# A hybrid SSD, mLSTM and PEER layer on one core: the order of loads, evacuations, sample rows and closing norms at the seams between its stages

## What is computed

```python
proj = einsum('bld,dc->blc', x, w_in)              # one projection for all parts
z_s, xbc, dt_pre, u_m, v_m, o_m, i_pre, f_pre = split(proj)
xbc, new_ssd_conv = causal_conv(xbc, st_ssd_conv)  # 4 taps, then SiLU
y_s, h_new = ssd_scan(...)                         # chunks of 128 tokens, 16 heads of 64
y_s = rms_norm((y_s + d_skip * xs) * silu(z_s), ssd_norm_g)
u_c = silu(causal_conv(u_m, st_mconv)); q, k = u_c @ w_mq, u_c @ w_mk
num = att @ v + w_inter * (q @ c)                  # mLSTM, 4 heads of 256
den = att.sum + w_inter * (q @ n);  h = num / max(|den|, exp(-m_t))
h_m = sigmoid(o_m) * (layer_norm_per_head(h) * mlstm_norm_g)
mix = concat([y_s, h_m]) @ w_out
x1 = layer_norm(ALPHA * x + mix, ln1_g, ln1_b)
# PEER: 8 heads; two top-16 lists of 128 keys each, top 16 of their sums
#       = 16 experts of 16384 for each token and head, with softmax gates
hid = gelu(einsum('td,thkd->thk', x1, take(u, eidx)))
out = einsum('thk,thkd->td', gate * hid, take(v, eidx))
x2 = layer_norm(ALPHA * x1 + out, ln2_g, ln2_b)    # y; all updated states are outputs too
```

## Time and profile before

| what | us |
|---|---|
| runs of the kernel before | 3408.26, 3424.15, 3424.18 (median 3424.15) |
| the profiled execution | 3417.68, of it span 3415.8 |
| TensorE busy | 3118.2 (91%) |
| VectorE busy | 2546.0 (75%) |
| GpSimd busy | 1710.7 (50%) |
| ScalarE busy | 933.5 (27%) |
| moved by DMA | 1074.44 MB, 315 GB/s over the span |

### The profile page before, as it was taken

One profiled execution on the slowest core, in us unless ns is written; L12 is line 12 of the kernel. 1 busy time (PEld: TensorE's weight loads), 2 busy tenths in 40 slices (PEclk: granted clock), 3 DMA queues, 4 the chain that ended last, 5 costly groups with the idle time before them and its releaser, 6 DMA issues.

```text
span 3415.8 us, 42585 instructions
## 1 busy us (share of the span) xinstructions
PE 3118.2 (91%) x13811; PEld 2060.5 (60%) x13811; DVE 2546.0 (75%) x5375; ACT 933.5 (27%) x2140; POOL 1710.7 (50%) x1420
## 2 busy tenths in 40 slices
PE   8998999998888888889877658999999999999998
PEld 8997887787333233333244336767667766776774
DVE  6672044888397889998889977777777777777777
ACT  3212222665111121121178771111111111111111
POOL 3231221443036777777754556555555555555553
PEclk9999999999899999999989788999999999999999
DMA  4325465677568999999989999999999999999996
GB/s 147 98 70 171 155 222 191 228 266 286 205 205 314 358 379 373 389 380 358 369 323 348 338 351 392 391 385 395 372 386 396 369 387 378 392 402 388 391 394 240
DMA packets 385759, 1074.44 MB, mean 315 GB/s; under 512 B 55688, under 2 KB 145576, under 8 KB 379280
## 3 DMA queue, kind: packets, MB, share of 16 engines
q0 software_dynamic: 186624, 679.56, 52.5%
q1 hardware_dynamic: 149104, 309.77, 25.3%
q10 hardware_dynamic: 49824, 82.58, 6.5%
HBM read 978.55 MB, written 93.08 MB: 314 GB/s over the span
## 4 chain that ended last, share of the span: by engine, by line
PE 45%; DVE 11%; DMA 9%; issue 5%; POOL 2%; ACT 1%; SPq 0%; DVEq 0%; POOLq 0%; ACTq 0%
PE PB L2260 18%; PE PB L2247 14%; DMA vbf<-in_peer_v,gixv 5%; PE PB L2223 4%; PE PB L2287 3%; PE PB L2236 3%; DVE ub L1916 3%; DMA x1d<-in_peer_u 3%; PE PB L2205 1%; DMA ub<-in_peer_u,gix 1%; POOL vbf L1646 1%; DVE ohb L1863 1%; POOL ub L1646 1%; DVE oha L1861 1%; PE PB L2331 1%
## 5 line engine op out<-in xcount | busy, mean ns | idle before, releaser
L1646 POOL DMA_INDIRECT ub<-in_peer_u,gix x640 | 696.3, 1088 | 725.8 <-DVE hid L1916 525.5
L2260 PE MATMUL PB<-vbd,wd 128*128 128x512 f32 x1536 | 685.0, 596 | 0.0
L2247 PE MATMUL PB<-xds,uts 128*128 128x384 f32 x3072 | 569.5, 340 | 0.0
L2247 PEld LDWEIGHTS PB<-xds,uts 128*128 128x128 f32 x3072 | 531.8, 189 | 0.5 <-issue 0.5
L1646 POOL DMA_INDIRECT vbf<-in_peer_v,gix x340 | 396.4, 1166 | 167.1 <-issue 98.0
L2260 PEld LDWEIGHTS PB<-vbd,wd 128*128 128x128 f32 x1536 | 284.1, 192 | 309.6 <-issue 309.6
L2287 PE MATMUL PB<-vbf,dg 128*64 128x512 f32 x1200 | 319.1, 655 | 96.9 <-DMA vbf<-in_peer_v,gixv 92.2
L1646 POOL DMA_INDIRECT vbf<-in_peer_v,gixv x300 | 324.6, 1082 | 156.4 <-issue 85.0
L1877 DVE TENSOR_TENSOR uts<-PB,uts 128x512 fp32r<-128x512 f32 x256 | 175.6, 686 | 303.0 <-ACT uts L2093 302.7
L1916 DVE CUSTOM_DVE_ANT_0 ub<-ub,x1g 128x1024 f32<-128x1024 f32 x257 | 312.9, 1221 | 47.2 <-DMA ub<-in_peer_u,gix 37.8
L2093 ACT CAST uts<-PB 128x512 fp32r<-128x512 f32 x256 | 149.9, 586 | 646.9 <-PE PB L2236 635.3
(11 more groups left out here) (400 smaller groups left out, 5030.4 us busy)
## 6 DMA issues: line engine op xcount, KB each, us to landing
vbd<-in_peer_v SPq DMA_DIRECT2D x128, 512.0 KB, 6.9
x1d<-in_peer_u SPq DMA_DIRECT2D x96, 512.0 KB, 9.3
gd_d<-stag ACTq DMA_DIRECT2D x12, 2048.0 KB, 9.6
gbd<-gd_d SPq DMA_DIRECT2D x16, 1536.0 KB, 18.9
ubd<-in_peer_u SPq DMA_DIRECT2D x32, 512.0 KB, 10.1
wtr<-in_w_tok SPq DMA_DIRECT2D x6, 2048.0 KB, 9.2
tok_d<-stg ACTq DMA_DIRECT2D x48, 256.0 KB, 2.0
rb_e<-rows_d SPq DMA_DIRECT2D x8, 1536.0 KB, 10.7
```

The lines of the kernel that those rows point to most:

```text
L1646: pool.indirect_dma_start(out=buf, out_offset=None, in_=a[table], in_offset=bass.IndirectOffsetOnAxis(ap=index, axis=0)).then_inc(done, 16)
L2247: last = T.matmul(PB[:, 6, 0:TD], uts[:, b % 2, ul, k, :], xds[:, xl, k, :], start=(k, n) == (0, 0), stop=(k, n) == (KD - 1, 2))
L2260: last = T.matmul(PB[:, 2 * d + n, :], wd[:, b % 2, d * CH:(d + 1) * CH], vbd[b % 8][:, n * 512:(n + 1) * 512], start=b == 0, stop=b == NB ...
```

## The change

- **Projection:** SyncE issues the first two w_ch loads after the seventh piece of x. ScalarE's channel loop is put in another order: a half's evacuation stands ahead of the other half's SiLU.
- **Scan, samples:** one masked copy of the queries, `qsm`, makes `sample_num` give only sample n's row and zeros elsewhere, and VectorE adds the eight results into one tile, `numr` (`sample_sum`). The row stores, `num_d` and its load are gone. The samples' SSD part is gated, squared and scaled in channel layout in rounds 0 and 3; the mLSTM part is normalised in 4 x 32 partitions after the loop; both go to `mixt_d` as one store, over zeros stored in round 0. Ten loads instead of five precede `sample_start`.
- **Scan, chunk 0:** `mt0` holds all 16 rows and is loaded in round 3; all of chunk 0's mix is computed before the barrier. x, gain, bias, the first mix group of chunk 1 and the first four pieces of the score weights (`wp0`) are loaded there too, into tiles that keep their place in the next stage.
- **PEER, head:** rows 0 to 2 of chunk 1's mix stand ahead of the transposes; VectorE's constants stand behind the first norm; the other loads of `wp` are interleaved with the mix groups.
- **PEER, end:** a tile's sum comes out of the operation that makes it (`accum_out`); ScalarE makes the mean, and the variance by one Square pass; VectorE's norms are interleaved with the sums. Four of the samples' v gathers stand ahead of the last slots, eight small loads bring their x1 rows, and their product runs in four column groups.

The diff, cut to its core:

```diff
@@ projection, SyncE
-                    for q in range(2):
-                        sp.dma_start(wcr[q][:, :, :], a["w_ch"][q, :, :, :]).then_inc(s_w[q], 16)
                     for k in range(KD):
                         free(sp, s_xl, k - NX + 1)
                         sp.dma_start(xst[k % NX], a["x_t"][:, k, :]).then_inc(s_x[k % NX], 16)
+                        if k == KD - 2:
+                            for q in range(2):
+                                sp.dma_start(wcr[q][:, :, :], a["w_ch"][q, :, :, :]).then_inc(s_w[q], 16)
@@ projection, ScalarE (chan_out: evacuation and its two stores; chan_silu: SiLU and its two stores)
+                    chan_out(0, 0)
+                    for i in steps(act, NCT // 2 - 1):
+                        chan_out(i, 1)
+                        chan_silu(i, 0)
+                        chan_out(i + 1, 0)
+                        chan_silu(i, 1)
+                    chan_out(NCT // 2 - 1, 1)
+                    for q in range(2):
+                        chan_silu(NCT // 2 - 1, q)
@@ scan, SyncE, round 3 and the end
+                if i == 3:
+                    sp.wait_ge(s["stored"], 16)
+                    sp.dma_start(mt0[:, :, :], mixt_d[0]).then_inc(s["mt0"], 16)
...
+            sp.wait_ge(s["dve_mix"], NCH)
+            sp.dma_start(x1e[:, :], a["x_tok"][0:CH, :]).then_inc(s["x0"], 16)
+            sp.dma_start(g1e[:, :], a["ln1_g"].partition_broadcast(P)).then_inc(s["x0"], 16)
+            sp.dma_start(mte[:, 0, :, :], mixt_d[1, :, 0:4, :]).then_inc(s["mt1"], 16)
+            for j in range(4):
+                sp.dma_start(wp0[:, j, :, :], wp_d[j]).then_inc(s["wp0"], 16)
@@ scan, TensorE
-                pe.wait_ge(ss["ld"], 16 * 5)
+                pe.wait_ge(ss["ld"], 16 * 10)
...
+            first_mix(0, 4)
+            sample_num(NCH - 1, 0)
+            first_mix(4, 6)
             mix_transposes(pe, P, NCH - 1)
+            pe.wait_ge(ss["mix"], 1)
...
+            first_mix(6, 16).then_inc(s["mix0"], 1)
@@ scan, ScalarE, end
+            act.dma_start(mixt_d[NCH, :, :, 0:B], mixs[:, :, :], allow_slow_non_contiguous=True).then_inc(ss["stored"], 16)
@@ scan, VectorE
+            V.memset(onesq[:, :], 1.0)
+            for tile in (qsm, numr, orow, grow):
+                V.memset(tile[:, :], 0.0)
+            V.memset(emr[:, :], 0.0).then_inc(ss["zeroed"], 1)
             V.memset(v1[:, :, DK:DK + 1], 1.0).then_inc(s["setup"], 1)
...
+            def sample_sum(n, bank=2):
+                dve.wait_ge(ss["num"], n + 1)
+                if n:
+                    dve.wait_ge(ss["numc"], n)
+                V.tensor_tensor(numr[:, :], numr[:, :], PB[:, bank, 0:DK], ALU.add).then_inc(ss["numc"], 1)
@@ PEER, SyncE
-                load_mt(0, 3)
-                load_x(0)
...
-                for j in range(NHC):
+                sp.sem_inc(s["xr"], 16)
+                sp.sem_inc(s["gl1"], 16)
+                sp.sem_inc(s["gl2"], 16)
+                sp.sem_inc(s_mt[0], 16)
+                for j in range(4, 8):
                     load_wp(j)
                 load_mt(1, 1)
+                for j in range(8, 12):
+                    load_wp(j)
+                load_mt(1, 2)
+                for j in range(12, 16):
+                    load_wp(j)
                 load_x(1)
@@ PEER, TensorE
-                pe.wait_ge(s_wo[3], 16)
-                for j in range(12, 16):
-                    mix(0, j)
+                pe.sem_inc(s["mixg"], 1)
+                for j in range(3):
+                    mix(1, j)
                 transposes(0)
...
-                        for n in range(NSMP):
-                            pe.wait_ge(s_vs[n], 16)
+                        for r in (1, 0):
+                            for g in range(4):
+                                pe.wait_ge(s_vs[4 * r + g], 16)
                             for x in range(2):
+                                for g in range(4):
+                                    last = T.matmul(PB[32 * g:32 * g + 2, 6 + x, :], wgs[:, 4 * r + g, 0:2], (ub if r else vbf)[:, g, x * 512:(x + 1) * 512],
+                                                    start=r == 1, stop=r == 0, tile_position=(0, 32 * g))
@@ PEER, VectorE, end (last_norm: reciprocal and two scalar_tensor_tensor)
+                def last_sum(n, x, psum):
+                    V.scalar_tensor_tensor(x, x, ALPHA, psum, ALU.mult, ALU.add, accum_out=ends[:, n, 0:1]).then_inc(s["ends_sum"], 1)
...
                 for d in range(ND):
                     dve.wait_ge(s["g2"], NBLK + d)
+                    last_sum(1 + d, x1d[:, d, :], two(2 * d))
+                    if d == 1:
+                        last_norm(0, acc[GATHERED - 1])
+                last_norm(1, x1d[:, 0, :])
+                dve.wait_ge(s["xsr"], 16 * NSMP)
                 dve.wait_ge(s["go"], 1)
+                last_sum(1 + ND, x1[:, :], two(6))
+                for d in range(1, ND):
+                    last_norm(1 + d, x1d[:, d, :])
+                last_norm(1 + ND, x1[:, :])
@@ PEER, ScalarE, end
+                    S.activation(ends[:, n, 0:1], ends[:, n, 0:1], ACT.Copy, scale=-1.0 / D).then_inc(s["ends_mean"], 1)
+                    act.wait_ge(s["ends_mean"], 2 * n + 1)
+                    S.activation(work[:, 0:D], x, ACT.Square, bias=ends[:, n, 0:1], accum_out=ends[:, n, 1:2]).then_inc(s["ends_mean"], 1)
+                    act.wait_ge(s["ends_mean"], 2 * n + 2)
+                    S.activation(ends[:, n, 1:2], ends[:, n, 1:2], ACT.Sqrt, scale=1.0 / D, bias=epsc[:, :]).then_inc(s["ysq"], 1)
```

More of the change, by code:

```diff
@@ L650, in build @@
             wo = late.enter_context(nc.sbuf_tensor("wo", [P, 16, D], f32))
-            mt0 = late.enter_context(nc.sbuf_tensor("mt0", [P, 12, CH], f32))
+            wp0 = late.enter_context(nc.sbuf_tensor("wp_first", [P, 4, KD, NK], f32))
+            late.enter_context(nc.sbuf_tensor("late_gap", [P, MIX_GAP], f32))
+            first = [late.enter_context(nc.sbuf_tensor(n, shape, f32))
+                     for n, shape in (("mt", [P, 2, 4, CH]), ("x1", [P, D]), ("x1T", [P, KD, CH]), ("gb1", [P, D]), ("gb2", [P, D]))]
         with ExitStack() as ctx:
-            build_scan(nc, a, o, ctx, sem, PB, ident, two, wo, s_wo, s_pre, pre, mt0, cht_d, chs_d, ych_d, tok_d, rows_d, rows_s_d, mixt_d)
+            build_scan(nc, a, o, ctx, sem, PB, ident, two, wo, s_wo, s_pre, pre, wp0, first, wp_d, cht_d, chs_d, ych_d, tok_d, rows_d, rows_s_d, mixt_d)
         end_phase()
@@ L891, in sample_start @@
             def sample_start():
-                pe.wait_ge(ss["ld"], 16 * 5)
+                pe.wait_ge(ss["ld"], 16 * 10)
+                for j in range(8):
+                    last = T.transpose(PB[:, 4, j * B:(j + 1) * B], z_s.rearrange("b j n -> b (j n)")[:, j * P:(j + 1) * P], ident[0:B, 0:B])
+                last.then_inc(ss["z_turned"], 1)
                 for k in range(KT):
@@ L973, in _ @@
                     sample_turn()
+                    T.matmul(PB[:, 3, 320:384], onesq[:, :], ysq[:, :, :].rearrange("p a b -> p (a b)"), start=True, stop=True).then_inc(ss["ysum"], 1)
                 pe.wait_ge(s["pool_xdec"], i + 1)
@@ L1242, in _ @@
                     dve.wait_ge(s["pe_" + done], i + 1)
+                    if i == 0 and half == 0:
+                        dve.wait_ge(ss["pad"], 16)
                     for h in (2 * half, 2 * half + 1):
@@ L1271, in build_peer @@
     X = mybir.AxisListType.X
-    PB, ident, two, sem, wo, s_wo = (L_[k] for k in ("PB", "ident", "two", "sem", "wo", "s_wo"))
+    PB, ident, two, sem, wo, wp0 = (L_[k] for k in ("PB", "ident", "two", "sem", "wo", "wp0"))
+    mt, x1, x1T, gb1, gb2 = L_["first"]
     mixt_d, wp_d = (L_[k] for k in ("mixt_d", "wp_d"))
@@ L1632, in _ @@
                         load_xs(4)
+                        sp.wait_ge(s["x1t"], NP)
+                        for n in range(NSMP):
+                            sp.dma_start(x1[32 * (n % 4) + n // 4:32 * (n % 4) + n // 4 + 1, :], x1_d[SEQ + n:SEQ + n + 1, :]).then_inc(s["xsr"], 16)
                 for n in range(len(x1s), NSMP):
@@ L1878, in u_low @@
                                     uts[:, b % 2, 0, 4 * x:4 * x + 4, :].rearrange("p k e -> p (k e)").bitcast(f32), ALU.subtract).then_inc(s["utl"], 1)
+                for step in range(6):
+                    norm1(0, step)
+                dve.wait_ge(s["x1"], 1)
+                V.tensor_copy(x1g_a[:, :], x1[:, :]).then_inc(s["x1c"], 1)
+                dve.wait_ge(s["x1c"], 1)
                 dve.wait_ge(s["iou"], 1)
@@ L2270, in _ @@
                     score(0, i)
-                for j in range(16):
+                for j in range(3, 16):
                     mix(1, j)
```

336 lines of the change are left out of this document (169 added, 167 removed).

## The result

The changed kernel takes 3381.1 us in the median of four runs (3374.4 to 3390.1) against 3421.9 of the kernel before beside it (four runs, 3408.3 to 3424.2): a ratio of 0.9882 [0.9852, 0.9913], 40.8 us less. The forecast was 3376, within 3356 to 3402. The profiled execution took 3379.5 us, its span 3377.6, so 38.2 less than the profiled one of before, where the sum had said 44.9.

What follows compares the result with a forecast made beforehand. Two long stages, gathers (DMA engines 0.93 busy) and dense blocks (TensorE), 2439 us together, were taken as untouched; gains at four seams sum to 44.9 us, giving 3372.8 or 3379.3, said as 3376, range 3356 to 3402.

Steps and rivals of the forecast that it cites:

- ScalarE's order, both terms (5.8 and 7.1): Channel loop: the 5.8 us evacuation wait goes whole; at the loop's end an earlier first peer-weight copy gains 7.1 us.
- start of the scan: Scan's first chunk: memsets 1.4, small transposes and sum 1.5, waiting for loads 1; together 4 us lost, bounds 2 and 12.
- end of the scan: Scan's end: TensorE ends at 872.8, peer stage begins at 873.9, 10.5 us earlier; bounds 11 gained and 9 lost.
- head of the PEER stage: Peer stage's start: VectorE's first operation on x comes 0.4 us after it instead of 13.25, 12.9 us gained, no range.
- clock of the scores: Peer stage's head: mix rows fill the norm's time, so the scores run at full clock; 3 us gained, bounds 0 and 4.
- tail: After VectorE's last rows: cheaper sums and norms, statistics on ScalarE, samples' product early; span ends 8 us sooner.
- TensorE's waits fall to about 10: Sign in the first 300 us: TensorE's waits fall from 24.7 us to about 10.
- If the barrier waits for a store: Sign of error at the scan's end: the barrier was expected to open on TensorE, with stores done by 867.
- rival A: Scan's end: 2048 pieces of 32 bytes hold the barrier until 893, 19.5 us late; gain 25, about 3396; chance 0.10.
- rival B: Tail: column groups don't overlap in the last product, so the tail gains only 0.5 us: 3384; chance 0.07.
- Rival C: Gather stage lengthens by 37 us and gives the gain back: about 3411, no change; chance 0.08.
- D: Gather and dense stages: gathers land later because SyncE's loads are in a new order; slower, say 3445; chance 0.05.

Runs made afterwards that it cites:

- e1: Changed kernel with ScalarE's old order in the channel loop (evacuation and SiLU of one half after the other): 3395.2 us, ratio 0.9931 to the kernel before.
- e2: Changed kernel with ScalarE's 14 row stores put ahead of the last SiLU of the channel loop: 3368.5 us, ratio 0.9847.
- c3: The kernel before, unaltered, run once more for a second profile: 3423.2 us in one run.
- c2: The changed kernel, unaltered, run once more for a second profile: 3371.2 us, ratio 0.9852 to the kernel before.
- e8: Changed kernel with the scan's new VectorE memsets put behind the memset that releases TensorE, ScalarE and GpSimd: 3393.0 us in one run.
- e6: Changed kernel with the samples' mix stored in 128 pieces of 512 bytes, in a buffer that nothing reads: 3403.0 us in one run.
- e7: Changed kernel with the samples' mix stored twice, the second time in the same 2048 pieces of 32 bytes: 3396.2 us in one run.
- e4: Changed kernel with no row of chunk 1's mix ahead of the first transposes, instead of three: 3369.5 us in one run.
- e3: Changed kernel with the last samples' product in one column group, all 32 passes one after the other: 3386.5 us in one run.
- e5: Changed kernel with one row of chunk 1's mix ahead of the first transposes, instead of three: 3393.0 us in one run.
- c4: The kernel before with ScalarE's new order in the channel loop alone: 3403.9 us against 3420.1, ratio 0.9952.

## Why the prediction was right, point by point

The time and the side were right; of the eight terms six were, one came out by another mechanism, and one was wrong. All are of the first pair of profiles.

| term | forecast | measured |
|---|---|---|
| start of the projection | 1.6 | 1.4 |
| ScalarE's order, both terms (5.8 and 7.1) | 12.9 | 12.8 |
| start of the scan | -4 | -3.1 |
| end of the scan | 10.5 | 9.2 |
| head of the PEER stage | 12.9 | 13.1 |
| clock of the scores | 3 | 0.4 |
| tail | 8 | 7.9 |
| gather and dense stage | 0 | -3.5 |
| sum | 44.9 | 38.2 |

- **The end of the channel loop: right sum, wrong cause.** I had TensorE restart 7.1 us sooner because the first peer-weight copy comes sooner. The copy did, but so did TensorE, and its wait stayed at 7.4. What paid were the 2.4 us wait, which I had as the lower bound, and 4.9 us of half clock behind it and behind the 5.8 us wait, which I had not priced at all: 2.4 + 4.9 = 7.3, less the 0.5 by which the copy's wait grew. I had read the clock behind a wait at the head of the PEER stage and not looked for it at this one. "TensorE's waits fall to about 10" was therefore wrong, 15.8. e1 gives back 12.7, 3.0 of it as slow clock; e2 shows what the copy's wait is worth when it is really taken away, 8.4.
- **One execution isn't the kernel.** The 5.8 us wait stands in all three traces of the old order (before, e1, c3), but the hold-up near 250 us differs: it cost a wait of 2.4 us in two of them and of 11.7 in c3. Between c3 and c2 the projection stage, without its start, differs by 24.4 us instead of 12.8. These 11.6 are most of the 17 by which the second pair of profiles lies further apart (55.3 us against 38.2). I had costed the order at what the trace showed and not asked what a longer hold-up of VectorE, of which the same trace holds a case, would do in either order.
- **Scan.** The memsets take 1.5 and cost 2.2 (e8), the rest being TensorE's clock behind its longer wait for them. The samples' sum costs nothing. The feared loads were not waited for.
- **Scan's end.** TensorE's work came out as counted. "If the barrier waits for a store" was named as a sign of error and came true, by 1.3 us instead of rival A's 19.5. A's pieces are cheap (e6, e7); scaling a load's 8.4 us by the number of pieces was the wrong bound.
- **The clock of the scores** was the term that failed. The passes did fall from 10.1 to 7.1; but the three rows end 3.2 us after x is ready, more than the 2.5 that I had named for them and put into the bound only, not into the sum; and before too the scores were faster in other executions (39.5 us from x to the first dot product in c3, 41.1 in the first profile). Net 0.4. e4 shows, in one trace, that the rows are still worth having, for the first gathers and not for the clock. My mark "some 37 us earlier than 940.7" took the second dot product for the first; the first went from 938.7 to 904.9, 33.8. The dense blocks, for which I had also written 37, start 27.5 us sooner (2031.3 instead of 2058.8): 33.8 less the 6.3 of the gather stage.
- **Tail.** 22.2 as written; rival B's price is 7.4 (e3). The table load was done at 3358.2, the root at 3358.5, VectorE reached its reciprocal at 3358.7: no drain beside the load shows, so the estimate of 7 by the Trainium skill (ScalarE: Activation LUTs, What ACT_TABLE_LOAD costs) doesn't hold here.
- **Rival C and D**: the gather stage took 1126.4, over the 1120 that I had named as a sign, but it took 1116 to 1123 in every other trace outside the group e5 to e8, with the stage of before and with that of the changed kernel. In that group it took 1142 to 1150 in four changed kernels, and no trace of before stands beside them.
- **The bounds.** The upper terms written above add up to 50.6 and not to 52, so the low end of the range is 1.4 too low. Nothing hangs on it.

## What to carry to other kernels

A wait of TensorE costs itself and, after a short wait in some executions only, up to about 3 us of half clock behind it: read the granted clock in windows of 2 us behind every wait before pricing its removal. On an engine that serves TensorE, put what TensorE waits for ahead of what waits for VectorE, and put DMA issues where the engine waits anyway: the first made the kernel about 16 us (10.6 to 22.2) faster by itself and its times less scattered, the second another 8.4 us at the start of the scan. Where one engine's operation can be blocked by another's, price an order by the worst place that it can fall, not by the one execution that was profiled.

## What the runs showed of the hardware that I had not expected

- One and the same wait of TensorE (2.33 us) was followed by a product of 3.72 us in some executions and of 5.40 in others; so was a wait of 1.19 us (scores of 7.13 or 8.84), and one of 2.4 us (a product of 1.90 in e1, of 2.96 in before). The Trainium skill (TensorE: Matmul & The Clock Gate, What's actually happening) says of a kernel's start that the number of slow matmuls varies from run to run of one kernel; here the same shows behind waits in the middle.
- While a GpSimd subtraction of 128x4096 ran (9.0 to 9.8 us), a VectorE step of 1.28 or 0.22 us took 10.1 or 8.9 us. Which step it catches differs between executions of one kernel.
- With a DMA share of 1.04 the issue of a store on ScalarE took 5.44 us, where it took 0.33 in the kernel before at a share of 0.31. That the share is the cause isn't tested.
- In the group e5 to e8 the gather stage took 1142 to 1150 us, in the other groups 1116 to 1126, while the dense stage (1318 to 1324) and the tail (22.1 to 22.4) were as long as elsewhere. It isn't the chip alone: c4 ran later on the same chip, and its gather stage took 1121.8; the kernel before took 3440.5 us beside e5 to e8 and 3420.1 beside c4. The cause stays open.
